# A fused decoder layer: small early work moved later, the second weight unit in halves, and the last expert pair in finer pieces

## The reference, cut to what matters

```python
h = rmsnorm(x, g_mix[l])
proj = h @ w_in[l]                       # 1024 x 2816: q, k, v of the mixers A, B, C, D
...                                      # A block-sparse, B differential, C stick-breaking, D sliding window
merged = sigmoid(h @ w_gate[l, 0]) * (branches[0] @ w_br[l, 0])
for i in range(1, 4):
    merged = merged + sigmoid(h @ w_gate[l, i]) * (branches[i] @ w_br[l, i])
x = x + merged @ w_o[l]
x = x + hierarchical_moe(rmsnorm(x, g_ffn[l]), ...)   # silu(xb @ w1[e]) * (xb @ w3[e]) @ w2[e]
return rmsnorm(x, g_final)
```

## Time and profile before

| | |
|---|---|
| time, 3 runs | 717.66, 717.75, 717.78 us (median 717.75) |
| profiled execution, its own time | 719.13 us |
| its span, first to last instruction | 717.3 us |
| PE busy | 685.7 us, 96% of the span |
| DVE, ACT, POOL busy | 34%, 27%, 1% |
| DMA | 243.56 MB, mean 340 GB/s |
| chain that ended last | PE 63%, DMA 22%, SPq 6%, DVE 5%, ACT 2% |
| mean granted TensorE clock | 0.990 |

### The profile page before, as it was taken

The page is one execution under the profiler, slowest core; times in us unless marked ns, Lnnn a source line. Parts: engine busy times, 40 slices in busy tenths (PEclk is TensorE's granted clock), DMA queues, the critical chain, the costliest instruction groups (busy, mean ns, idle before and its releaser), DMA issues.

```text
span 717.3 us, 9888 instructions
## 1 busy us (share of the span) xinstructions
PE 685.7 (96%) x4042; PEld 401.6 (56%) x4042; DVE 245.9 (34%) x526; ACT 192.0 (27%) x304; POOL 4.2 (1%) x8
## 2 busy tenths in 40 slices
PE   8999999999999999999999999999989899898995
PEld 6899887777777874344344344344334343442432
DVE  7463556766567673121121121122121020210212
ACT  5551565598563521100100100001000010000112
POOL 0000000000000000000000000000000000000000
PEclk9999999999999999999999999999999999998998
DMA  8899631374439978999999999999999999999992
GB/s 308 284 273 286 215 117 59 118 259 152 176 118 343 406 307 292 409 428 426 426 427 426 425 428 426 429 426 428 428 429 426 429 427 428 424 428 429 414 399 104
DMA packets 46125, 243.56 MB, mean 340 GB/s; under 512 B 10192, under 2 KB 13448, under 8 KB 33800
## 3 DMA queue, kind: packets, MB, share of 16 engines
q1 hardware_dynamic: 45640, 241.45, 84.6%
q0 software_dynamic: 448, 1.59, 0.7%
HBM read 241.96 MB, written 1.07 MB: 339 GB/s over the span
## 4 chain that ended last, share of the span: by engine, by line
PE 63%; DMA 22%; SPq 6%; DVE 5%; ACT 2%; issue 2%; POOLq 0%; DVEq 0%; ACTq 0%
PE bank L1713 21%; DMA unit<-in_w 20%; PE bank L1768 8%; PE bank L1386 7%; PE bank L1387 7%; PE bank L1388 7%; SPq L548 5%; PE bank L1691 4%; DMA unit<-in_w_in 2%; DVE low L332 2%; PE bank L1780 1%; PE bank L1781 1%; PE bank L1742 1%; PE bank L1478 1%; ACT high L327 1%
## 5 line engine op out<-in xcount | busy, mean ns | idle before, releaser
L1713 PE MATMUL bank<-unit,xT 128*64 128x512 f32 x1024 | 230.8, 604 | 14.0 <-DMA unit<-in_w 12.3
L1713 PEld LDWEIGHTS bank<-unit,xT 128*64 128x64 f32 x1024 | 76.0, 139 | 153.5 <-issue 147.1
L1768 PE MATMUL bank<-unit,hidT 128*64 128x512 f32 x480 | 106.3, 595 | 0.0
L1386 PE MATMUL bank<-high,hT_hi 128*128 128x512 f32 (+2 forms) x208 | 79.8, 384 | 2.4 <-DVE low L332 2.4
L1387 PE MATMUL bank<-low,hT_hi 128*128 128x512 f32 (+2 forms) x208 | 77.3, 372 | 0.0
L332 DVE TENSOR_TENSOR low<-unit,high 128x2048 fp32r<-128x2048 f32 (+1 forms) x34 | 70.7, 2099 | 11.4 <-ACT high L327 11.4
L1768 PEld LDWEIGHTS bank<-unit,hidT 128*64 128x64 f32 x480 | 33.1, 137 | 61.5 <-issue 60.0
L1388 PE MATMUL bank<-high,hT_lo 128*128 128x512 f32 (+2 forms) x176 | 65.1, 370 | 0.0
L327 ACT ACTIVATE high<-unit 128x2048 fp32r<-128x2048 f32 (+1 forms) x34 | 58.9, 1756 | 8.4 <-PE bank L1388 5.1
L1263 DVE TENSOR_TENSOR y_lo<-bank,y_hi 128x512 fp32r<-128x512 f32 x30 | 20.7, 691 | 94.1 <-ACT y_hi L793 94.1
L1691 PEld LDWEIGHTS bank<-pick,hk 128*128 128x128 bf16 x768 | 44.4, 98 | 13.5 <-issue 12.2
(11 more groups left out here) (252 smaller groups left out, 688.0 us busy)
## 6 DMA issues: line engine op xcount, KB each, us to landing
unit<-in_w SPq DMA_DIRECT2D x86, 2048.0 KB, 30.1
unit<-in_w_gate SPq DMA_DIRECT2D x8, 2048.0 KB, 9.9
unit<-in_w SPq DMA_DIRECT2D x12, 1024.0 KB, 26.6
unit<-in_w SPq DMA_DIRECT2D x14, 512.0 KB, 9.0
unit<-in_w_in SPq DMA_DIRECT2D x3, 2048.0 KB, 15.9
unit<-in_w_br SPq DMA_DIRECT2D x4, 1024.0 KB, 6.0
unit<-in_w_o SPq DMA_DIRECT2D x2, 2048.0 KB, 10.6
unit<-in_w_in SPq DMA_DIRECT2D x6, 512.0 KB, 7.6
```

What stands on the lines that cost most here:

```text
L1386: mm(dst, a_hi, b_hi, start=first, stop=False)
L1713: last = mm(bank[4 + w][g * CAP:(g + 1) * CAP, :], xT[:, k, g * CAP:(g + 1) * CAP], rhs, start=(k == 0), stop=(k == KD - 1))
L1768: last = mm(bank[6 + n][g * CAP:(g + 1) * CAP, :], hidT[:, c, g * CAP:(g + 1) * CAP], rhs[:, c, n * BANK:(n + 1) * BANK], start=(c == 0), ...
```

## The change

Six edits. (1) Unit 1 is loaded in two DMAs of 1 MB, and ACT's first half waits for the first alone. (2) DVE's `dvec` goes from before the readouts of unit 0 to behind the readout of block 5; the constants and the lambda work go behind the conversions of units 4 and 5; ACT's exponential goes behind the second half of the conversion that follows unit 3's readouts; PE starts with 23 instead of 18 idle-time matmuls. (3) The wait for the readout of bank 4 goes behind the first scores. (4) In step 7 DVE converts its weight half ahead of the head squares. (5) The last quarter of the last branch product is split, one half ahead of the turning of row tile 0. (6) The last pair: 12 pieces for 9, the combine of the pair before moved ahead of up (w3), hidden rows computed, turned and copied in two halves, and the output DMAs in the order that the diff lists.

```diff
-LAST_PIECES = ((0, 0, 0, 0, 4), (0, 0, 0, 4, 8), (0, 2, 0, 0, 4), (0, 2, 0, 4, 6), (0, 2, 0, 6, 8),
-               (0, 4, 0, 0, 4), (0, 4, 1, 0, 2), (0, 4, 1, 2, 3), (0, 4, 1, 3, 4))
+LAST_PIECES = ((0, 0, 0, 0, 4), (0, 0, 0, 4, 8),
+               (0, 2, 0, 0, 2), (0, 2, 0, 2, 4), (0, 2, 0, 4, 6), (0, 2, 0, 6, 7), (0, 2, 0, 7, 8),
+               (0, 4, 0, 0, 2), (0, 4, 0, 2, 4), (0, 4, 1, 0, 2), (0, 4, 1, 2, 3), (0, 4, 1, 3, 4))
...
@@ high_part
+            elif xi == 1 and piece == 0:
+                act.wait_ge(s["second_half"], 16)
...
@@ SP
+                if u == 1:
+                    sp.dma_start(dst[:, 0:4, :], src[:, 0:4, :]).then_inc(s["second_half"], 16)
+                    dst, src = dst[:, 4:, :], src[:, 4:, :]
                 sp.dma_start(dst, src).then_inc(s_unit[u % RING1], 16)
...
-            for t in range(NT):
-                for n in range(2):
-                    sp.wait_ge(*((s[("half0", "half1")[t]], 1) if n == 0 else (s["scaled"], t + 1)))
+            for t, n, ready, count in ((0, 1, s["scaled"], 1), (1, 0, s["half1"], 1), (1, 1, s["scaled"], 2), (0, 0, s["half0"], 1)):
+                sp.wait_ge(ready, count)
...
@@ ACT
-            act.wait_ge(s["lamx"], 1)
-            nc.scalar.activation(lam[:, 2:4], lam[:, 0:2], ACT.Exp).then_inc(s["lame"], 1)
...
+                if u == 3:
+                    act.wait_ge(s["lamx"], 1)
+                    nc.scalar.activation(lam[:, 2:4], lam[:, 0:2], ACT.Exp).then_inc(s["lame"], 1)
...
@@ ACT, experts
+                if last:
+                    for half, (ready, done) in enumerate(((s["last_half"], s["last_half"]), (z["hTp"], z["hT"]))):
+                        act.wait_ge(ready, 2 if half == 0 else p + 1)
+                        nc.scalar.activation(hidT[:, 2 * half:2 * half + 2, :].rearrange("p c q -> p (c q)"),
+                                             bank[4 + half][:, 0:TOK], ACT.Copy).then_inc(done, 1)
...
@@ DVE: the same instructions as before, now in three functions
+            def bias_vectors():
+                dve.wait_ge(s["small"], 16 * 9)
+                dve.wait_ge(s["table"], 1)
+                nc.vector.tensor_tensor(dvec[:], bank[7][0:12, 0:MAP], bmask[:], ALU.add).then_inc(s["dvec"], 1)
...
@@ DVE, the loop over units
+                    if i == 5:
+                        bias_vectors()
                 for half in range(2 if u < 5 else 0):
                     low_part(dve, nc.vector, u + 2, half)
+                if u == 2:
+                    constants()
+                elif u == 3:
+                    weight_of_difference()
...
                 if st == 7:
+                    low_part(dve, nc.vector, 10, 1)
                     head_squares_summed()
-                if st == 7:
-                    low_part(dve, nc.vector, 10, 1)
                     head_norms_end()
...
@@ PE
-            keep_warm(18)
+            keep_warm(23)
...
-            for b in (0, 1, 4):
+            def read_out(b):
...
+            for b in (0, 1):
+                read_out(b)
             scores_ahead(0)
+            read_out(4)
...
             branch(D_, 2)
+            branch(3, 3, [0])
             pe.wait_ge(s["mrg"], 14)
             turn_tile(0, merged, s["mTps"])
-            branch(3, 3)
+            branch(3, 3, [1])
...
@@ PE, the last pair
                     turn_picks(main, p)
+                    combine(main, p - 1, [0])
                     up(1, main, p, slots, here)
-                    combine(main, p - 1, [0])
-                    turn_hidden(main, p)
+                    turn_half(main, p, 0)
                     combine(main, p - 1, [1])
+                    turn_half(main, p, 1)
+                    pe.wait_ge(s["last_half"], 3)
+                    pe.wait_ge(main["gs"], p + 1)
+                    down_last(main, p, slots, here, 0, range(2))
                     pe.wait_ge(main["hT"], p + 1)
-                    pe.wait_ge(main["gs"], p + 1)
-                    down_last(main, p, slots, here, 0, range(CE))
+                    down_last(main, p, slots, here, 0, range(2, CE))
```

More of the change, by code:

```diff
@@ L1245, in gathered, with hidden @@
                                     ALU.mult).then_inc(z["xT"], 1)
-            def hidden(z, p, first=False):
+            def hidden(z, p, first=False, last=False):
                 dve.wait_ge(z["sg"], p + 1)
@@ L1270, in experts @@
                     picks(main, p + 1, p + 1)
-                hidden(main, p, first)
+                hidden(main, p, first, last)
                 if not last:
@@ L1724, in turn_hidden, with turn_half @@
                 last.then_inc(z["hTp"], 1)
+            def turn_half(z, p, half):
+                pe.wait_ge(*((z["hid"], p + 1) if half else (s["last_half"], 1)))
+                for c in range(2):
+                    c_th = hid[:].rearrange("p (q c) -> p c q", c=CE)[:, 2 * half + c, :]
+                    last = nc.tensor.transpose(bank[4 + half][:, c * P:(c + 1) * P], c_th, ident)
+                last.then_inc(z["hTp"] if half else s["last_half"], 1)
             def turn_picks(z, p):
@@ L1861, in here @@
                         def here(r, step):
-                            for w in (r, r + 1) if step == 0 else ():
-                                pe.wait_ge(s_over_unit[w], 16 * q + 16)
+                            if step == 0:
+                                pe.wait_ge(s_over_unit[r // 2], 32 * q + 32)
                         pe.wait_ge(over["P"], q + 1)
```

50 lines of the change are left out of this document (28 added, 22 removed).

## The result

The changed kernel takes 721.05 us (median of 13 executions, 718.51 to 722.65) against 717.75 of the kernel before (717.42 to 720.18). The ratio is 1.0041, 95% interval 1.0034 to 1.0048: slower by 0.41%, 2.9 us. The forecast was 721.9, between 718.8 and 724.2. The profiled execution of after took 721.05 by its own time, its span is 719.2 us, its mean granted clock 0.985 (717.3 and 0.990 before).

What follows compares the result with a forecast made beforehand. Expert-weight transfers were taken to set the pace from 287 us, PE before it; terms 3.2 + 2.3 - 0.5 + 0.5 - 0.3 - 0.3 - 0.8 = +4.1 us on the median 717.75 gave 721.9 us, range 718.8 to 724.2.

Steps and rivals of the forecast that it cites:

- Unit 1 in halves: PE's waits of 0.54 and 0.52 us for unit 1 go: -1.06 us, bounds 0 and -1.06.
- `dvec` behind unit 2: PE stands 5.1 us at block 7 for `dvec`; with unit 1's gain and two vanishing waits, +3.2 us.
- The clock after the stand: PE's clock falls to half after its wait at block 7: +2.3 us, bounds 0 and 3.4.
- Rest of the small work: Constants, lambda and exponential moved later cost nothing; up to 3.2 us if their cover were gone.
- five more idle-time matmuls: At PE's start they fill waiting time and cost nothing, at most 1.1 us.
- Bank 4: The first scores hide PE's wait of 0.56 us for ACT: -0.5 us, bounds -0.56 and 0.
- Step 7: PE's 0.78 us wait goes, but later head squares delay root, scaling and turning: net +0.5 us, bounds -0.78 and +0.6.
- Branch product in two parts: Part of it fills PE's 0.80 us wait ahead of the turning at 227.69: -0.3 us, bounds -0.7 and 0.
- Last pair: Down comes 0.4 us later if PE is late, up to 1.0 sooner if transfers are; taken as -0.3 us.
- output: First output DMA goes at 711.83 instead of 712.83, the last lands sooner: -0.8 us, bounds -0.4 and -1.0.
- Front delay passes on one for one: A delay or gain of PE before 270 us moves the full transfer stretch and the end equally.
- no stand: Rival: unit 2 lands below 25 us, PE does not wait at block 7; 714.5 us, chance 0.12.

Runs made afterwards that it cites:

- filled stand: The changed kernel with 18 matmuls of constants by constants on PE ahead of its wait for `dvec` at block 7: 719.90 us, ratio 1.0030.
- kernel with `dvec` behind: The kernel before with only `dvec` moved behind the low part of unit 2 and the readout of block 5: 720.48 us, ratio 1.0043.
- pure delay: The kernel before with 24 matmuls of constants by constants on PE ahead of its wait for `dvec` at block 7: 722.95 us, ratio 1.0072.

## Why the prediction was right

Forecast +4.1 us, measured +2.9 by the ratio (2.4 to 3.4). By its own steps:

- **Unit 1 in halves, -1.06.** Right in kind, too small: -1.5 to -1.6 in "a to b". The step took the shown idle time for the whole cost.
- **`dvec` behind unit 2, the term that decides.** Right: same chain, same waits. The stand was 4.37 us, not 5.1: unit 2 landed 1.0 us sooner, and PE came to block 7 at 32.1 instead of 32.5. The step took the landing at 30.17 for fixed, as "a measured one"; it is one draw from a spread of at least 27.7 to 30.2, and was at its late end.
- **The clock after the stand, +2.3.** 2.5 by the filled stand and by the rows (27 matmuls at a pitch of 0.213 in place of 0.118 us). The step's choice of the middle between two ups was lucky in its size but rested on the right rows. The Trainium skill (TensorE: Matmul & The Clock Gate, Part 1), which it cited, puts the penalty at half of the throttled time. The trace agrees roughly: PE worked at the slow clock for 5.7 us, half of which is 2.9, against 2.5. The throttling began about 1 us before PE resumed. In the kernel with `dvec` behind, though, the clock held through the stand and fell 1.5 us after it, which the step did not foresee.
- **Rest of the small work, 0.** Right in the changed kernel, since the stand covers it. That this part is worth 1.3 us without the stand, the prediction did not see; it called the vanishing waits a by-product of the stand. The **five more idle-time matmuls** were costed at nothing, too low: point a comes at 10.1 to 10.8 us in the six kernels with 18 of them (mean 10.40) and at 10.1 to 11.4 in the eight with 23 (mean 10.91), and in all eight no wait shows between them and the first turning, so they do not only fill time. About +0.5 us, from profiles that differ in other things too; it was not tried alone.
- **Bank 4, -0.5.** -0.65.
- **Step 7, +0.5.** +0.45, with the mechanism as told.
- **Branch product in two parts, -0.3.** -0.1: "d to e" is 108.97 to 109.06 with it and 109.07 to 109.15 without. The wait of 0.80 is gone, and most of it is lost again before the gather; 0.32 us of it shows as a new wait of PE, at 234.01, ahead of the output product.
- **Last pair, -0.3, and output, -0.8.** -0.35 and -0.65 alone, both with intervals that reach to zero. Together, "e to end" has a mean of 450.05 in the eight kernels with both and 451.89 in the four with neither, -1.8 us, or -1.5 without the two profiles with a late remainder. Why this is more than the two edits' -1.0 alone stays open.
- **Front delay passes on one for one.** The pure delay shows that nothing is absorbed: 3.9 us in the stretch came out as 5.1 (4.2 to 6.2).

The stretches add up, with the means for point a and the tail: 0.5 - 1.5 + 5.3 + 0.4 - 0.1 - 1.8 = +2.8 us. How close that is to 2.9 is partly luck: the 5.3 is of one profile and moves with the landing of unit 2. The forecast was too high by the shorter stand, unit 1's larger gain and the tail's. Its rival "no stand", with 714.5 us below a landing of 25 us, was met when the landing was moved to 24.7: 713.88.

The best kernels are the changed one with `dvec` ahead and the old step 7 (713.4 us, 0.65% faster than before) and the one with the small loads behind unit 2. Both together, and with 18 idle-time matmuls, were not run.

## What to carry to other kernels

On an in-order engine a tiny instruction costs what stands ahead of it: a 0.54 us addition behind a conversion that waits for a transfer held PE for 4.4 us, and the slow clock behind it cost 2.5 more. Before small work is moved later, look at what it moves behind, whether that waits for a DMA, and how far the landing varies from one execution to the next; and if a weight transfer is late, look first at the small loads that are issued ahead of it. Single edits of half a microsecond are read from stretches between fixed points of one engine, which repeat to about 0.1 us here where no transfer is waited for, long before the total time can tell them apart. Choose the two points so that the work moved stays between them: the last pair looked 0.6 us faster between two points that its moved matmuls had left.

## What the runs showed of the hardware

- The DMA of 2 MB that loads unit 2, with the same bytes ahead of it in its queue, landed between 27.7 and 30.2 us in thirteen profiled executions.
- The granted clock fell to 0.50 after a wait of 1.83 us, and not in it but 1.5 us after PE had resumed; it stayed there 3.2 us. After the wait of 4.37 us it had fallen before PE resumed and stayed for another 5.7 us.
- A wait of PE costs about 0.26 us more than its row shows, where matmuls of 256 columns follow each other.
- In two of fourteen profiles the last remainder of the output DMAs came 1.4 and 2.3 us late, in either order of issue.
